# Where PE waits for VectorE's dots, and the order of the second stream in a two-layer transformer kernel

## The chip, the cores and the metric

One core of one Trainium2 chip runs the whole program in one launch. The metric is device time in microseconds (us), the median of several runs. The engines are named as the profile names them: PE is TensorE's matmul, PEld its weight load, DVE is VectorE, ACT is ScalarE, POOL is GpSimd, SP is SyncE, which here only issues DMAs. A "unit" is one 128 x 1024 block of weights in fp32, 512 KB.

## The reference, cut to what matters

The input is 256 tokens x and 256 context tokens ctx, of width 1024. Two layers of a first block are followed by two layers of a second one. The change lies between layer 0's MLP and layer 1's projection of the first block:

```python
mx = (silu(c) @ ada_w[i] + ada_b[i])[:, None, :]      # shift, scale, gate for x
mc = silu(c_ctx) @ ada_w[i] + ada_b[i]                # the same for ctx
hx = hx + gx2 * _mlp(_modulate(hx, norm2_g[i], sx2, cx2), mlp_w1[i], mlp_w2[i])
hc = hc + gc2 * _mlp(_modulate(hc, norm2_g[i], sc2, cc2), mlp_w1[i], mlp_w2[i])
# layer 1
ax = _modulate(hx, norm1_g[i], sx1, cx1)              # rms norm * (1 + scale) + shift
ac = _modulate(hc, norm1_g[i], sc1, cc1)
q, k, v = split(ax @ w_in)
cq, ck, cv = split(ac @ w_in)                         # layer 1 has no queries of ctx
q, k = rope(q), rope(k)
```

The queries of layer 1 are needed for x alone, its keys for x and ctx. Rope multiplies a tile by cosines and adds a copy with swapped rows times sines.

## The kernel before, in words

**Weights.** 284 units stream through four slots. SP loads a unit into `raw`; ACT rounds it to `whi` (L578); DVE subtracts to get the rest, `wlo` (L923); PE multiplies in three passes (L1663 to L1665: high x high, low x high, high x low), so that a tile of eight blocks is 24 matmuls. ACT and DVE each make unit u+3 in a step called `ahead(u)`, at a place in their own program that is written out by hand. Every engine works through its own list in order, and semaphores tie the lists together: `w_lo` counts finished units, `w_used` units that PE is through with.

**Two streams.** The activations `Hh`, `Hl` hold 512 columns, 256 of x ("first stream") and 256 of ctx ("second stream"). At the end of layer 0's MLP the last three tiles (`halves`, L1791 on) are done for x first, then for ctx, so that the norm of x can begin early. With halves (i, v), v = 0 for x and 1 for ctx, PE's order is (0,0), (1,0), (2,0), (0,1), then `sums_of(n, 0)` (L1769, the sums of squares of x, into PSUM bank 7), (1,1), `spread_of(n, 0)` (L1787), (2,1). The halves write to the banks 0, 1, 4 and 5, 2, 1.

**Dots.** Since layer 0's MLP leaves DVE time, DVE computes the modulation rows (`silu(c) @ ada_w`) there: `ada_dot` passes of 128 x 1024 (L997) whose elementwise product goes to PSUM banks 6 and 7. PE may not write to bank 7 before they are over. The last of them is followed by `ada_sums` (L1012), which raises `ada_ready`. PE waits for it before the first of the halves.

**Behind the dots.** DVE adds each finished half into X (L1319), ACT squares it (L628), POOL adds the squares (L1546, semaphore `sqx_used`); `sums_of(n, 0)` needs two of these adds and a last square. Then DVE scales (L1046, M tile), ACT adds the shift and rounds (`hi_x` L638 for x, `hi_c` L643 for ctx), DVE makes the low part (L1056), semaphores `low_x` and `nlo`, tile by tile, k = 0 to 7.

**Layer 1's projection.** It has 16 tiles in the order `L1_ORDER` (L103): 0 to 7 are queries of 256 columns, 8 to 15 keys of 512. `first_stream` (L1808) takes the first three tiles together as x's norm arrives; two more queries follow, then PE waits for all eight `nlo` (L2092) and does key 8. ACT evacuates tile i (`evac`, L672) from one of four PSUM banks into one of two buffers of `wk1` (`turned`), for which it waits until rope i-2 is over (`rope_out`); POOL multiplies by the cosines into the second half of the same buffer (L1619), DVE swaps, multiplies by the sines and adds (L1172, L1173, L1175). `L1_SECOND` says at which steps i of the 16 the second stream's tiles are made, on ACT and on DVE, and `L1_ROPES` at which steps DVE does which ropes. At step i ACT does `ahead`, the second stream's part, `evac(i)`; DVE does `ahead`, the second stream's part, the ropes.

The functions printed here are those that the change touches.

Of the kernel before, what the change touches and what calls it, by code (L numbers as in the profile page):

```python
# [28 lines left out]
ALU = mybir.AluOpType  # L29
# [5 lines left out]
KT = D // P  # L35
N = 256
# [5 lines left out]
QUARTERS = 4  # L42
# [23 lines left out]
U_L1 = U_L0_MLP + MLP_UNITS  # L66
L1_FM = 16
# [7 lines left out]
ADA_GROUPS = KT  # L75
# [24 lines left out]
OUT_BANKS = ((1, 2, 4), (5, 0, 3))  # L100
MLP_BANKS = ((0, 1, 4), (5, 2, 1))

L1_ORDER = (0, 1, 2, 3, 4, 8, 9, 10, 5, 11, 6, 12, 7, 13, 14, 15)  # L103


def program(nc, wall, aall, const, prm, xin, rpb, ali, out):
    with ExitStack() as top:
# [109 lines left out]
        class Norm:  # L217


            def __init__(self, src, n, T, width, streams, dst, eps=1e-6, keep=None, ready=None,  # L220
                         direct=False):
                self.src, self.n, self.T, self.width, self.eps = src, n, T, width, eps
                self.streams = streams
                self.dst = dst
                self.keep = keep
                self.ready = ready
                self.direct = direct

                self.pair = None
# [17 lines left out]
        norms = {}  # L247
# [41 lines left out]
        class Proj:  # L289
# [1 line left out]
            outs = 0  # L291
            ropes = 0

            def __init__(self, u0, tiles, high=False):
                self.u0, self.tiles = u0, tiles

                self.high = high
                self.o0, self.r0 = Proj.outs, Proj.ropes
                Proj.outs += len(tiles)
                Proj.ropes += sum(t.rope is not None for t in tiles)  # L300
# [2 lines left out]
                return (self.o0 + i) % 4 + (4 if self.high else 0)  # L303

            def turned(self, r):
                return wk2[:, 2 + r % 2, :] if self.high else wk1[:, r % 2, :]

            def swapped(self, r):
                return MO[:, r % 2, :] if self.high else wk1[:, 2 + r % 2, 0:N]
# [15 lines left out]

        L1_ROPES = ((), (), (0,), (1,), (2,), (3, 4)) + tuple((i - 1,) for i in range(6, L1_FM))
        L1_SECOND = (range(0, 4), range(4, 6), range(6, 8)) + (range(0),) * (L1_FM - 3)


        ROPE = {"q": (0, 128, C_COS, C_SIN), "m": (64, 128, C_COSM, C_SINM), "r": (0, 128, C_COSM, C_SINM),
# [6 lines left out]
        def v_place(o0, t):  # L339
# [4 lines left out]
            if o0 < V_L1 + 16:  # L344
# [1 line left out]
            return ps[:, (o0 + t) % 4, 0:N]  # L346

        p_l1 = Proj(U_L1, [Tile(256, "q", Q1[:, i, :], None, 0.125) if i < 8
                           else Tile(512, "q", K1[:, i - 8, 0:N], K1[:, i - 8, N:2 * N]) for i in L1_ORDER])

        def b2_tile(i):
            if i < 3 or 6 <= i < 8:
# [219 lines left out]
        def _(act):  # L572
# [73 lines left out]
            def last_halves(u, n):  # L646


                square(n, HALVED - 1)
                for k in range(HALVED, KT):  # L650
                    square_x(n, k)
                for k in range(HALVED, KT - 1):
                    ahead(u + k - HALVED + 1)
                    square_c(n, k)
                hi_x(n, 0)
                hi_x(n, 1)
                square_c(n, KT - 1)
                for k in range(2, KT):
                    hi_x(n, k)

            def evac(pr, i):
                t, o = pr.tiles[i], pr.o0 + i
                act.wait_ge(sem("w_used"), pr.u0 + i + 1)
                bank = ps[:, pr.bank(i), :]
                if t.rope is None:
                    act.activation(t.dst, bank[:, 0:t.T], ACT.Copy, scale=t.scale).then_inc(sem("proj_out"), 1)
                    return
                r = pr.rope_index(i)
                lo, hi, _, _ = ROPE[t.rope]
                if r >= 2:  # L670
                    act.wait_ge(sem("rope_out"), r - 1)
                ins = act.activation(pr.turned(r)[lo:hi, 0:N], bank[lo:hi, 0:N], ACT.Copy, scale=t.scale)  # L672
                if t.rest is not None:
                    rest = bank[0:64, 0:N] if t.rope == "m" else bank[:, N:2 * N]
                    ins = act.activation(t.rest, rest, ACT.Copy, scale=t.scale)
                ins.then_inc(sem("proj_out"), 1)
# [142 lines left out]


            for i in range(L1_FM):
                ahead(U_L1 + i)
                for k in L1_SECOND[i]:
                    hi_c(norms["l1a"], k)
                evac(p_l1, i)
# [86 lines left out]
        def _(dve):  # L912
# [251 lines left out]
            def rope(pr, i):  # L1164
                t = pr.tiles[i]
                r = pr.rope_index(i)
                lo, hi, _, sines = ROPE[t.rope]
                dve.wait_ge(sem("proj_out"), pr.o0 + i + 1)
                if r >= 2:
                    dve.wait_ge(sem("rope_out"), r - 1)  # L1170
                turned, swapped = pr.turned(r)[lo:hi, :], pr.swapped(r)[lo:hi, :]
                link(dve.stream_shuffle(swapped, turned[:, 0:N], SWAP))  # L1172
                link(dve.tensor_tensor(swapped, swapped, cst[lo:hi, sines:sines + N], ALU.mult))  # L1173
                dve.wait_ge(sem("rope_cos"), r + 1)
                dve.tensor_tensor(t.dst, turned[:, N:2 * N], swapped, ALU.add).then_inc(sem("rope_out"), 1)  # L1175

            def steps(pr, lo, hi):

# [344 lines left out]
        def _(pool):  # L1523
# [84 lines left out]
            def cosines(pr):  # L1608

                for i, t in enumerate(pr.tiles):  # L1610
                    if t.rope is None:
                        continue
                    r = pr.rope_index(i)
                    lo, hi, c, _ = ROPE[t.rope]
                    pool.wait_ge(sem("proj_out"), pr.o0 + i + 1)
                    if r >= 2:
                        pool.wait_ge(sem("rope_out"), r - 1)
                    turned = pr.turned(r)[lo:hi, :]
                    pool.tensor_tensor(turned[:, N:2 * N], turned[:, 0:N], cst[lo:hi, c:c + N], ALU.mult)\  # L1619
                        .then_inc(sem("rope_cos"), 1)  # L1620

            pool.wait_ge(sem("mhalf_set"), 1)
# [37 lines left out]
        def _(pe):  # L1660
# [129 lines left out]
            def halves(n, units, banks, x, free):  # L1790

                for v in range(2):
                    for i, u in enumerate(units):
                        if v == 0:
                            pe.wait_ge(sem("w_lo"), u + 1)
                        free(i, v)
                        for k in range(KT):
                            ins = mm3(ps[:, banks[v][i], 0:N], wtile(u % SLOTS, P * k, P),
                                      (x[0](k)[:, N * v:N * v + N], x[1](k)[:, N * v:N * v + N]), k == 0, k == KT - 1)
                        ins.then_inc(sem("w_used" if v else "half_used"), 1)  # L1800
                        if v == 1 and i == 0:
                            sums_of(n, 0)
                        if v == 1 and i == 1:
                            spread_of(n, 0)
# [23 lines left out]
                        if k == KT - 1:  # L1828
                            ins.then_inc(sem("w_used"), 1)

            def project(pr, lo, hi, x, kts=KT, ready=None):

                groups = [range(i, i + 1) for i in range(lo, hi)]
                if ready is not None:
                    groups = [range(0, TOGETHER)] + groups[TOGETHER:]
                for group in groups:
                    for i in group:
                        pe.wait_ge(sem("w_lo"), pr.u0 + i + 1)  # L1840
                        if pr.o0 + i >= 4:
                            pe.wait_ge(sem("proj_out"), pr.o0 + i - 3)
                    for k in range(kts):
                        if group[0] == 0 and ready is not None:
                            pe.wait_ge(sem("nlo"), ready + k + 1)
                        for i in group:
                            T = pr.tiles[i].T
                            ins = mm3(ps[:, pr.bank(i), 0:T], wtile((pr.u0 + i) % SLOTS, P * k, P),
                                      (x[0](k)[:, 0:T], x[1](k)[:, 0:T]), k == 0, k == kts - 1)
                            if k == kts - 1:  # L1850
                                ins.then_inc(sem("w_used"), 1)
# [128 lines left out]
            def mlp(u0, h0, T, ready, first=None, last=None):  # L1980
                def quarter(it, head=None, tail=None):
# [31 lines left out]

                    if tail is not None:
                        def free(i, v):
                            if v == 0 and i == 0:

                                pe.wait_ge(sem("ada_ready"), ADA_GROUPS + QUARTERS)
                            elif v == 1 and i == 1:
                                pe.wait_ge(sem("mlp_added"), 8 * it + (1 + h0 + HALVED))  # L2020
                            elif v == 1 and i == 2:
                                pe.wait_ge(sem("added_x"), 3 * tail.pair + 2)

                        halves(tail, range(u0 + 16 * it + 8 + HALVED, u0 + 16 * it + 16),
                               MLP_BANKS, (lambda k: HIDh[:, k, :], lambda k: HIDl[:, k, :]),
                               free)
# [62 lines left out]
            pe.wait_ge(sem("added_x"), 4)  # L2089
            first_stream(norms["l1a"], range(U_L1, U_L1 + TOGETHER), [(p_l1.o0 + i) % 4 for i in range(TOGETHER)], Hx)  # L2090
            project(p_l1, TOGETHER, L1_ORDER.index(8), Hx)
            pe.wait_ge(sem("nlo"), norms["l1a"].h0 + KT)  # L2092
            project(p_l1, L1_ORDER.index(8), L1_FM, Hx)
            for c in range(4):
                if c == 3:
                    pe.wait_ge(sem("rope_out"), p_l1.r0 + 16)
# [231 lines left out]
```

## Time and profile before

| | us |
|---|---|
| median of 3 runs | 1394.72 (1392.08 to 1395.4) |
| the profiled execution's own time | 1393.3 |
| its span in the trace | 1391.4 |
| PE busy in the span | 1322.6 (95%) |
| DVE, ACT, POOL busy | 993.6 (71%), 671.0 (48%), 193.1 (14%) |

The profile comes from one execution. Its span is 1.9 us shorter than that execution's own time, and that time is 1.4 us under the median of the runs. Times of single events are given in us from the span's start. PE is busy for 95% of the span; the page lists the rest as waits of single engines, and these are what a change to order can reach.

### The profile page before, as it was taken

The page shows a single profiled execution, that of the slowest core. Times are in us where ns is not written, and L with a number is a line of the kernel's source. Part 1 is how long each engine was busy: PE and PEld are TensorE (multiplying, and loading weights), DVE is VectorE, ACT ScalarE, POOL GpSimd, SP SyncE. Part 2 cuts the span into 40 slices and gives each one's busy share as a digit, 9 for nine tenths or more (in the row PEclk, how much of TensorE's full clock was granted, in tenths as well). Part 3 has the DMA queues.
Part 4 walks back from the last instruction along what each step waited for, and adds up shares of the span by engine and source line. Part 5 has one row for each costly group of instructions (what it writes and reads, how often), then busy time and mean ns, then how long its engine had stood idle before and what let it go on. Part 6 is the DMA issues. An engine that isn't in the chain of part 4 may idle for free. (4 is left out here: it accounts for less than half of the span.)

```text
span 1391.4 us, 24946 instructions
## 1 busy us (share of the span) xinstructions
PE 1322.6 (95%) x9374; PEld 1169.3 (84%) x9374; DVE 993.6 (71%) x1724; ACT 671.0 (48%) x1354; POOL 193.1 (14%) x280
## 2 busy tenths in 40 slices
PE   7999999999999999789999899999999989899987
PEld 6786679888888888688886899999899968899967
DVE  5698778898878878767439465565665976765974
ACT  4427743622414325144238464466455555465473
POOL 0101213000000000112006600000220016020034
PEclk8999999999999999899999999999999999899998
DMA  8782133567867868624320345655374533454511
GB/s 300 268 249 98 47 111 132 183 225 247 300 239 270 296 218 281 218 77 137 96 86 1 120 138 167 196 193 177 120 262 158 176 106 108 143 180 159 165 60 46
DMA packets 67666, 234.99 MB, mean 169 GB/s; under 512 B 7280, under 2 KB 12400, under 8 KB 67312
## 3 DMA queue, kind: packets, MB, share of 16 engines
q1 hardware_dynamic: 67568, 233.67, 49.8%
q8 instruction: 63, 1.03, 0.3%
q14 instruction: 35, 0.29, 0.1%
HBM read 232.59 MB, written 1.05 MB: 168 GB/s over the span
## 5 line engine op out<-in xcount | busy, mean ns | idle before, releaser
L923 DVE TENSOR_TENSOR wlo<-raw,whi 128x1024 fp32r<-128x1024 f32 x284 | 350.5, 1235 | 176.4 <-ACT whi L578 170.7
L578 ACT ACTIVATE whi<-raw 128x1024 fp32r<-128x1024 f32 x284 | 299.5, 1055 | 240.0 <-PE ps L1665 239.7
L1663 PE MATMUL ps<-Hh,whi 128*128 128x256 f32 (+1 forms) x896 | 304.7, 340 | 8.5 <-DVE Hl L1056 3.4
L1664 PE MATMUL ps<-Hl,whi 128*128 128x256 f32 (+1 forms) x896 | 301.0, 336 | 0.0
L1665 PE MATMUL ps<-Hh,wlo 128*128 128x256 f32 (+1 forms) x896 | 301.0, 336 | 0.0
L1663 PEld LDWEIGHTS ps<-Hh,whi 128*128 128x128 f32 x896 | 170.4, 190 | 31.2 <-issue 6.4
L1665 PEld LDWEIGHTS ps<-Hh,wlo 128*128 128x128 f32 x896 | 170.2, 190 | 19.2
L1663 PE MATMUL ps<-HIDh,whi 128*128 128x256 f32 (+1 forms) x536 | 177.8, 332 | 8.8 <-DVE ada L1012 8.8
L1664 PEld LDWEIGHTS ps<-Hl,whi 128*128 128x128 f32 x896 | 170.6, 190 | 18.3
L1663 PE MATMUL ps<-Gh,whi 128*128 128x256 f32 x624 | 178.1, 285 | 3.9 <-DVE Gl L1130 3.9
L1664 PE MATMUL ps<-HIDl,whi 128*128 128x256 f32 (+1 forms) x536 | 177.5, 331 | 0.0
L1665 PE MATMUL ps<-HIDh,wlo 128*128 128x256 f32 (+1 forms) x536 | 177.4, 331 | 0.0
L1664 PE MATMUL ps<-Gl,whi 128*128 128x256 f32 x624 | 176.9, 283 | 0.0
L1665 PE MATMUL ps<-Gh,wlo 128*128 128x256 f32 x624 | 176.8, 283 | 0.0
L997 DVE CUSTOM_DVE_ANT_0 ps<-aring,SB 128x1024 f32<-128x1024 f32 x112 | 141.3, 1261 | 2.6 <-DVE AC L997 0.3
L1663 PEld LDWEIGHTS ps<-Gh,whi 128*128 128x128 f32 x624 | 119.6, 192 | 5.0 <-issue 5.0
L1664 PEld LDWEIGHTS ps<-Gl,whi 128*128 128x128 f32 x624 | 119.6, 192 | 0.0
L1665 PEld LDWEIGHTS ps<-Gh,wlo 128*128 128x128 f32 x624 | 119.5, 192 | 0.0
L1663 PEld LDWEIGHTS ps<-HIDh,whi 128*128 128x128 f32 x536 | 102.9, 192 | 18.3 <-issue 9.2
L1664 PEld LDWEIGHTS ps<-HIDl,whi 128*128 128x128 f32 x536 | 102.9, 192 | 9.0
L1665 PEld LDWEIGHTS ps<-HIDh,wlo 128*128 128x128 f32 x536 | 102.9, 192 | 9.0
L696 ACT ACTIVATE wk<-ps,small 128x512 f32<-128x512 f32 (+2 forms) x160 | 84.2, 539 | 19.5 <-DVE small L1203 17.8
(251 smaller groups left out, 2041.5 us busy)
## 6 DMA issues: line engine op xcount, KB each, us to landing
raw<-wall SPq DMA_DIRECT2D x284, 512.0 KB, 4.2
aring<-aall SPq DMA_DIRECT2D x144, 512.0 KB, 4.6
AL<-ali SPq DMA_DIRECT2D x14, 192.0 KB, 5.2
X<-xin SPq DMA_DIRECT2D x2, 1024.0 KB, 7.4
BI<-rpb SPq DMA_DIRECT2D x4, 512.0 KB, 9.6
out<-X SPq DMA_DIRECT2D x4, 256.0 KB, 2.4
cst<-const SPq DMA_DIRECT2D x1, 960.0 KB, 8.3
par<-prm SPq DMA_DIRECT2D x1, 134.5 KB, 2.2
```

The costliest lines, as they stand in the source:

```text
L578: act.activation(whi[:, slot, :], raw[:, slot, :], ACT.Copy).then_inc(sem("w_hi"), 1)
L696: ins = act.activation(E[:, s % 2, r, c0:c0 + nk], ps[:, 2 * (s % 2) + r, c0:c0 + nk], ACT.Exp, bias=st[:, x:x + 1], accum_out=st[:, 4 + x ...
L923: dve.tensor_tensor(wlo[:, slot, :], raw[:, slot, :], whi[:, slot, :].bitcast(F32), ALU.subtract)\
L997: ins = dve.tensor_tensor_reduce(ps[:, 6:8, :].rearrange("p b n -> p (b n)"), w, SB[:, v, :], 1.0, start, ALU.mult, ALU.add, to)
L1663: pe.matmul(o, a[0], b[0], start=first, stop=False)
L1664: pe.matmul(o, a[0], b[1], start=False, stop=False)
L1665: return pe.matmul(o, a[1], b[0], start=False, stop=last)
```

## The change

It has two parts. First, PE's wait for `ada_ready` leaves the start of the halves and stands before `sums_of(n, 0)`. Second, layer 1's beginning is reordered: query 5 comes before key 8; ACT makes the high part of unit U_L1+3 behind x's `hi_x` tile k = 4, with the tiles 5 to 7 after it; the second stream's tiles are made at the steps 1 (two), 2 (two) and 3 (four) where they were made at 0 (four), 1 (two) and 2 (two); PE waits for them tile by tile within key 8; each tile is evacuated into its own place in Q1 or K1 and turned there, so that ACT's wait for rope i-2 goes, while the cosine product has still two buffers; and the ropes start at step 4 where they started at step 2.

```diff
-L1_ORDER = (0, 1, 2, 3, 4, 8, 9, 10, 5, 11, 6, 12, 7, 13, 14, 15)
+L1_ORDER = (0, 1, 2, 3, 4, 5, 8, 9, 10, 6, 11, 12, 7, 13, 14, 15)
...
             def turned(self, r):
+                if self.own:
+                    return self.tiles[r - self.r0].dst
                 return wk2[:, 2 + r % 2, :] if self.high else wk1[:, r % 2, :]
+
+            def cosined(self, r):
+                return wk1[:, r % 2, N:2 * N] if self.own else self.turned(r)[:, N:2 * N]
...
-        L1_ROPES = ((), (), (0,), (1,), (2,), (3, 4)) + tuple((i - 1,) for i in range(6, L1_FM))
-        L1_SECOND = (range(0, 4), range(4, 6), range(6, 8)) + (range(0),) * (L1_FM - 3)
+        L1_SECOND = (range(0), range(0, 2), range(2, 4), range(4, 8)) + (range(0),) * (L1_FM - 4)
+        L1_ROPES = ((), (), (), (), (0,), (1,), (2, 3), (4, 5), (6, 7)) + tuple((i - 1,) for i in range(9, L1_FM))
...
                 for k in range(2, KT):
                     hi_x(n, k)
+                    if n.pair == 1 and k == 4:
+                        ahead(u + 3)
...
-                if r >= 2:
+                if r >= 2 and not pr.own:
                     act.wait_ge(sem("rope_out"), r - 1)
...
             for i in range(L1_FM):
-                ahead(U_L1 + i)
+                if i:
+                    ahead(U_L1 + i)
...
-                dve.tensor_tensor(t.dst, turned[:, N:2 * N], swapped, ALU.add).then_inc(sem("rope_out"), 1)
+                dve.tensor_tensor(t.dst, pr.cosined(r)[lo:hi, :], swapped, ALU.add).then_inc(sem("rope_out"), 1)
...
-                    pool.tensor_tensor(turned[:, N:2 * N], turned[:, 0:N], cst[lo:hi, c:c + N], ALU.mult)\
+                    pool.tensor_tensor(pr.cosined(r)[lo:hi, :], turned[:, 0:N], cst[lo:hi, c:c + N], ALU.mult)\
...
                         if v == 1 and i == 0:
+                            if n.pair == 1:
+                                pe.wait_ge(sem("ada_ready"), ADA_GROUPS + QUARTERS)
                             sums_of(n, 0)
...
                         if group[0] == 0 and ready is not None:
                             pe.wait_ge(sem("nlo"), ready + k + 1)
+                        if second is not None:
+                            pe.wait_ge(sem("nlo"), second + k + 1)
...
                         def free(i, v):
-                            if v == 0 and i == 0:
-                                pe.wait_ge(sem("ada_ready"), ADA_GROUPS + QUARTERS)
-                            elif v == 1 and i == 1:
+                            if v == 1 and i == 1:
...
             project(p_l1, TOGETHER, L1_ORDER.index(8), Hx)
-            pe.wait_ge(sem("nlo"), norms["l1a"].h0 + KT)
-            project(p_l1, L1_ORDER.index(8), L1_FM, Hx)
+            project(p_l1, L1_ORDER.index(8), L1_ORDER.index(8) + 1, Hx, second=norms["l1a"].h0)
+            project(p_l1, L1_ORDER.index(8) + 1, L1_FM, Hx)
```

PE at the two places of the first part, before: the last tile of 512 columns ends, the halves begin; further down the sums stand behind the half (0,1). `HIDh` and `HIDl` are the MLP's hidden activations.

```order
2040 L1665 MATMUL ps<-HIDh,wlo 128x512
2041 L1663 MATMUL ps<-HIDh,whi 128x256 [waits ada_ready,w_lo]
2042 L1664 MATMUL ps<-HIDl,whi 128x256
...
2136 L1665 MATMUL ps<-HIDh,wlo 128x256
2137 L1769 MATMUL ps<-cst,RS 128x2 [waits sqx_used,modded]
2138 L1769 MATMUL ps<-cst,RS 128x2
```

and with the change:

```order
2040 L1677 MATMUL ps<-HIDh,wlo 128x512
2041 L1675 MATMUL ps<-HIDh,whi 128x256 [waits w_lo]
2042 L1676 MATMUL ps<-HIDl,whi 128x256
...
2136 L1677 MATMUL ps<-HIDh,wlo 128x256
2137 L1781 MATMUL ps<-cst,RS 128x2 [waits sqx_used,modded,ada_ready]
2138 L1781 MATMUL ps<-cst,RS 128x2
```

The wait for `ada_ready` has moved down by 96 matmuls; nothing else in this stretch has moved.

ACT from x's last `hi_x` tiles into layer 1's steps, before. `whi<-raw` is `ahead`, `Hh<-wk2 ... modded` the second stream, `wk1<-ps` (with the change `Q1<-ps`) the evacuation.

```order
326 L638 ACTIVATE Hh<-wk2,ada 128x256 [waits scaled_x] x6
327 L578 ACTIVATE whi<-raw 128x1024 [waits w_used,w_landed3]
328 L643 ACTIVATE Hh<-wk2,ada 128x256 [waits modded] x4
329 L672 ACTIVATE wk1<-ps 128x256 [waits rope_out,w_used]
330 L578 ACTIVATE whi<-raw 128x1024 [waits w_used,w_landed0]
331 L643 ACTIVATE Hh<-wk2,ada 128x256 [waits modded] x2
332 L672 ACTIVATE wk1<-ps 128x256 [waits rope_out,w_used]
333 L578 ACTIVATE whi<-raw 128x1024 [waits w_used,w_landed1]
334 L643 ACTIVATE Hh<-wk2,ada 128x256 [waits modded] x2
335 L672 ACTIVATE wk1<-ps 128x256 [waits rope_out,w_used]
```

and with the change:

```order
326 L647 ACTIVATE Hh<-wk2,ada 128x256 [waits scaled_x] x3
327 L587 ACTIVATE whi<-raw 128x1024 [waits w_used,w_landed3]
328 L647 ACTIVATE Hh<-wk2,ada 128x256 [waits scaled_x] x3
329 L683 ACTIVATE Q1<-ps 128x256 [waits w_used]
330 L587 ACTIVATE whi<-raw 128x1024 [waits w_used,w_landed0]
331 L652 ACTIVATE Hh<-wk2,ada 128x256 [waits modded] x2
332 L683 ACTIVATE Q1<-ps 128x256 [waits w_used]
333 L587 ACTIVATE whi<-raw 128x1024 [waits w_used,w_landed1]
334 L652 ACTIVATE Hh<-wk2,ada 128x256 [waits modded] x2
335 L683 ACTIVATE Q1<-ps 128x256 [waits w_used]
336 L587 ACTIVATE whi<-raw 128x1024 [waits w_used,w_landed2]
337 L652 ACTIVATE Hh<-wk2,ada 128x256 [waits modded] x4
```

One `whi` has moved up between x's tiles, the second stream's first group down behind the first evacuation, and its group of four is now the last.

DVE at the same place, with the change (before, one `wlo` stood at 791, the second stream in groups of 4, 2 and 2 behind it, and the first rope at 807, behind the third group):

```order
791 L935 TENSOR_TENSOR wlo<-raw,whi 128x1024 [waits w_hi] x2
792 L1058 SCALAR_TENSOR_TENSOR wk2<-X,SC,ps 128x256 [waits nlo,spread]
793 L1058 SCALAR_TENSOR_TENSOR wk2<-X,SC,ps 128x256 [waits nlo]
794 L1068 SCALAR_TENSOR_TENSOR Hl<-wk2,ada,Hh 128x256 [waits nhi] x2
795 L935 TENSOR_TENSOR wlo<-raw,whi 128x1024 [waits w_hi]
...
801 L1058 SCALAR_TENSOR_TENSOR wk2<-X,SC,ps 128x256 [waits nlo]
...
807 L935 TENSOR_TENSOR wlo<-raw,whi 128x1024 [waits w_hi]
808 L1184 STREAM_SHUFFLE wk1<-Q1 128x256 [waits rope_out,proj_out]
```

Two splits of weights stand in a row ahead of the second stream, the second of them waiting for ACT, with the whole second stream queued behind it.

## Rows read from the trace of the kernel before

**Rows 1.** The page: part 1, busy us of each engine; part 5, the dots' group, mean ns.

```profile
PE 1322.6 (95%) x9374; PEld 1169.3 (84%) x9374; DVE 993.6 (71%) x1724; ACT 671.0 (48%) x1354; POOL 193.1 (14%) x280
...
L997 DVE CUSTOM_DVE_ANT_0 ps<-aring,SB 128x1024 f32<-128x1024 f32 x112 | 141.3, 1261 | 2.6 <-DVE AC L997 0.3
```

**Rows 2.** PE's waits, 570 to 690: us in total, times, longest.

```profile
PE ps L1663 <- DVE ada L1012: 8.8, 1, 8.8
PE ps L1663 <- DVE Hl L1056: 3.0, 2, 2.6
```

**Rows 3.** Timeline of PE, 560 to 598: start, us, what, [idle before <-releaser].

```profile
573.71 0.39 PE L1665 MATMUL ps<-HIDh,wlo 128*128 128x512 f32 x1
582.90 0.55 PE L1663 MATMUL ps<-HIDh,whi 128*128 128x256 f32 x1 [8.80 <-DVE ada L1012]
...
588.75 0.28 PE L1663 MATMUL ps<-HIDh,whi 128*128 128x256 f32 x1
...
597.01 0.51 PE L1769 MATMUL ps<-cst,RS 128*128 128x2 f32 x4
```

**Rows 4.** Busy us (x instructions) of PE, PEld, DVE, ACT, POOL; granted clock; DMA.

```profile
574.00:582.90 8.90, 0.10 (x1) 0.03 (x1) 8.62 (x16) 1.61 (x2) 1.44 (x1) 0.75 0.72 249
582.90:588.60 5.70, 5.70 (x27) 5.70 (x28) 0.14 (x1) 0.00 (x0) 0.00 (x0) 0.50 0.00 0
...
604.40:624.30 19.90, 15.79 (x130) 15.39 (x130) 16.49 (x36) 10.47 (x20) 2.25 (x3) 1.00 0.27 89
624.30:678.00 53.70, 53.65 (x264) 44.52 (x264) 35.27 (x72) 19.26 (x33) 10.98 (x13) 1.00 0.41 134
```

**Rows 5.** Timeline of DVE, 573 to 589: a split, a dot, the sums, the first half.

```profile
573.13 1.22 DVE L923 TENSOR_TENSOR wlo<-raw,whi 128x1024 fp32r<-128x1024 f32 x1
...
576.37 2.11 DVE L997 CUSTOM_DVE_ANT_0 ps<-aring,SB 128x1024 f32<-128x1024 f32 x1
...
582.36 0.40 DVE L1012 TENSOR_TENSOR ada<-AC,par 128x4 f32<-128x4 f32 x4
588.47 0.48 DVE L1319 SCALAR_TENSOR_TENSOR X<-ps,ada,X 128x256 f32<-128x256 f32 x1 [5.71 <-PE ps L1665]
588.87 0.56 DVE L1023 SCALAR_TENSOR_TENSOR SC<-ada,par 128x8 f32<-128x8 f32 x3
```

**Rows 6.** Timeline of POOL and ACT: the last full add, then what follows the first half.

```profile
575.94 1.44 POOL L1540 TENSOR_TENSOR RS<-RS,wk 128x512 f32<-128x512 f32 x1 [4.00 <-ACT wk L605]
589.55 0.74 POOL L1546 TENSOR_TENSOR RS<-RS,wk 128x256 f32<-128x256 f32 x1 [12.16 <-ACT wk L628]
...
588.98 0.42 ACT L628 ACTIVATE wk<-X 128x256 f32<-128x256 f32 x1 [13.18 <-DVE X L1319]
```

**Rows 7.** Timeline of PE in layer 1: tile 3's first matmul, tile 4's, key 8's.

```profile
614.10 0.28 PE L1663 MATMUL ps<-Hh,whi 128*128 128x256 f32 x1
...
618.69 0.38 PE L1663 MATMUL ps<-Hh,whi 128*128 128x256 f32 x1 [1.58 <-DVE wlo L923]
...
624.35 0.50 PE L1663 MATMUL ps<-Hh,whi 128*128 128x512 f32 x1 [2.58 <-DVE Hl L1056]
```

**Rows 8.** Timeline of DVE there: splits, and the last low part between the first two.

```profile
611.50 1.23 DVE L923 TENSOR_TENSOR wlo<-raw,whi 128x1024 fp32r<-128x1024 f32 x1 [0.47 <-ACT whi L578]
...
616.19 0.49 DVE L1056 SCALAR_TENSOR_TENSOR Hl<-wk,ada,Hh 128x256 fp32r<-128x256 f32 x1 [0.18 <-ACT Hh L643]
617.41 1.23 DVE L923 TENSOR_TENSOR wlo<-raw,whi 128x1024 fp32r<-128x1024 f32 x1 [0.73 <-ACT whi L578]
...
621.22 1.23 DVE L923 TENSOR_TENSOR wlo<-raw,whi 128x1024 fp32r<-128x1024 f32 x1 [0.73 <-ACT whi L578]
```

**Rows 9.** Timeline of ACT: a high part released by PE; evacuation and high part.

```profile
597.27 1.06 ACT L578 ACTIVATE whi<-raw 128x1024 fp32r<-128x1024 f32 x1 [2.00 <-PE ps L1665]
...
616.06 0.37 ACT L672 ACTIVATE wk<-ps 128x256 f32<-128x256 f32 x1
616.33 1.05 ACT L578 ACTIVATE whi<-raw 128x1024 fp32r<-128x1024 f32 x1
```

More of the change, by code:

```diff
@@ L292, in program, with __init__ @@
             ropes = 0
-            def __init__(self, u0, tiles, high=False):
+            def __init__(self, u0, tiles, high=False, own=False):
                 self.u0, self.tiles = u0, tiles
+                self.own = own
                 self.high = high
@@ L348, in program @@
         p_l1 = Proj(U_L1, [Tile(256, "q", Q1[:, i, :], None, 0.125) if i < 8
-                           else Tile(512, "q", K1[:, i - 8, 0:N], K1[:, i - 8, N:2 * N]) for i in L1_ORDER])
+                           else Tile(512, "q", K1[:, i - 8, 0:N], K1[:, i - 8, N:2 * N]) for i in L1_ORDER], own=True)
         def b2_tile(i):
@@ L1829, in second_stream, with project @@
                             ins.then_inc(sem("w_used"), 1)
-            def project(pr, lo, hi, x, kts=KT, ready=None):
+            def project(pr, lo, hi, x, kts=KT, ready=None, second=None):
                 groups = [range(i, i + 1) for i in range(lo, hi)]
```

## The prediction

> **What bounds the kernel.** The page's first part shows PE busy for 1322.6 of 1391.4 us [rows 1]: the time is PE's work, its clock, and the few waits between. So I read PE's waits next, in the stretch that the change touches: one of 8.8 us for DVE's sums behind the dots, and shorter ones for DVE's low parts and splits [rows 2]. The timeline places them. PE's last matmul of 512 columns starts at 573.71, the halves at 582.90 [rows 3], just after DVE's sums, which start at 582.36 [rows 5]. The stretches show what the wait leaves behind: the granted clock, 1.00 (2.4 GHz) elsewhere, has a mean of 0.75 in the wait and is 0.50 (1.2 GHz) for the 5.70 us after it, in which 27 matmuls run [rows 4]. Last come layer 1's first tiles: tile 4 waits 1.58 us for its split, key 8 waits 2.58 us for the second stream [rows 7]. From 624.3 to 678.0 PE is busy for 53.65 of 53.70 us [rows 4], so whatever is saved before is kept there.
>
> **Part one, the moved wait.** Nothing else holds the halves at 574: the split of their last unit starts at 573.13 and takes 1.22 us [rows 5], and they write to no bank that the dots use. PE goes on one matmul of 512 columns later, 573.71 + 0.23 = 573.94 (53.65/264 us is the mean of mixed tiles; eight keys of 24 matmuls and three queries of 24 fit it at 0.234 and 0.120 us). Before the sums stand 96 matmuls of 256 columns. At full clock 96 - 27 = 69 of them took 597.01 - 588.75 = 8.26 us [rows 3, 4], 0.120 each, so all take 11.5 us and PE stands before its sums at 585.4.
>
> What is late next is DVE's chain. The sums of the dots end at 582.36 + 0.40 = 582.76 [rows 5], so `ada_ready`, now ahead of PE's sums, is up 2.7 us before PE gets there. But only then can DVE add its halves, and PE's sums need two of them squared and added by POOL. From rows: a half to the row scales 0.40, these 0.56 [rows 5]; a half's start to ACT's square 0.51, to POOL's add 1.08, which takes 0.74 [rows 5, 6]. The second half starts at 582.8 + 0.40 + 0.56 = 583.76 and its add is over at 583.76 + 1.08 + 0.74 = 585.6; the third half's square starts at about 584.7 and is over by then. PE starts its sums at 585.65, after a new wait of 0.2 us. They started at 597.01: **11.36 us**, of which 8.96 are the wait, 14.1 - 11.5 = 2.6 the low clock, less 0.2. All behind the sums (the spread, x's scaled tiles, the first stream) hangs on PE by the same order, and moves with it. The DMAs are no bound: in 582.90 to 588.60 their share is 0.00 [rows 4], so layer 1's first units have landed.
>
> POOL's two adds now run beside DVE's halves, with no row of the like before. If a half were held back for a whole add, the sums would start 0.74 later; if nothing, as above. I take the value above, since POOL's add begins only after the second half's start, and keep 0.74 for the range. For this a rule is at hand: a dot took 2.11 us from 576.37, where the mean is 1.26, beside POOL's add of 1.44 from 575.94 [rows 1, 5, 6]. The Trainium skill (SBUF — State Buffer, "SBUF: two separate sides") says that the pair of ports which DVE and GpSimd share is locked for a whole instruction, against DVE instructions with two SBUF inputs. The dot has two and agrees; a half reads X and a PSUM bank, so by the rule 0.2 stays, without it up to 0.9.
>
> **Part two, layer 1's start.** I keep the old clock here (all of it 11.36 earlier). Tile 3 starts at 614.10 [rows 7]. ACT's moved `whi` lies between `hi_x` tiles: it takes about 1.0 [rows 9] and delays the later ones by under 0.5, while PE asks for the last low part at 613.0 and DVE had it before its split at 611.50 [rows 8]; nothing.
>
> The next split, unit +4, sets the pace. ACT now evacuates tile 0 when the first stream is over for it. The last matmul of tile 0 starts at 614.10 - 7 x 0.12 = 613.27, that of tile 1 at 613.63; ACT starts 0.38 behind such a matmul (596.89 to 597.27) [rows 3, 9]. Evacuation at 613.65, `whi` at 614.01, the split 1.08 after (616.33 to 617.41) [rows 8, 9]: 615.09. From a split to the matmul that needs it is 1.28 (617.41 to 618.69) [rows 7, 8]. From one split to the next, with two tiles of the second stream, an evacuation and `whi` between, is 3.81 (617.41 to 621.22); with four tiles 5.91 (611.50 to 617.41) [rows 8]. A query takes 2.86, a key 5.63.
> - Tile 4: split ready 616.37, PE free 616.96: no wait (was 1.73 between slots, 1.58 of it idle).
> - Tile 5, a query: 615.09 + 3.81 + 1.28 = 620.18 against 619.82: waits 0.36.
> - Key 8: 622.71 + 1.28 = 623.99 against 623.04: waits 0.95 (was 2.73, 2.58 of it idle). Its last block is due at 623.99 + 7 x 0.70 = 628.9, and the last low part ends 5.18 after the split's start (611.50 to 616.68) [rows 8], at 627.9; no wait inside.
> - Key 9: 622.71 + 5.91 + 1.28 = 629.90 against 629.62: waits 0.28.
>
> Behind it DVE owes a split and one or two ropes a tile. Over the eleven tiles from 624.3 it is busy for 35.27 us [rows 4], 3.2 a tile; so the split for key 10 is there near 628.6 + 3.2 + 1.28 = 633.1 and needed at 635.5, and a key gives it 5.63 each. ACT's `rope_out` wait is gone, but PE was full there anyway: nothing. POOL's cosine products keep their two buffers: nothing, since their cover, the 5.63 - 3.2 = 2.4 us that DVE has left at each key, holds; without it a split would come late by one product at most, 0.74. So waits of 1.73 + 2.73 = 4.46 become 1.59: **2.87 us**.
>
> **Sum.** 11.36 + 2.87 = 14.2 us, against the profiled execution's own 1393.3: 1379.1. That execution is 1.4 under the median; the median becomes 1394.7 - 14.2 = **1380.5 us**. The runs before span 3.3 us, and under 0.3% (4.2 us) I would call no change.
>
> **Rivals.**
> - *The second part gives nothing* (0.14). The second stream begins later than before, and PE may again lose 4.46 us to splits and low parts at key 8. For it: PE waited on just these two. Against: the intervals above are of the same instructions. Only 11.4 remain: 1383.3.
> - *The clock falls at a short wait* (0.06). There are now four waits of 0.2 to 0.95 us in 45 us. Against it: two waits of 1.58 and 2.58 us left the granted clock at 1.00 [rows 4, 7]. A low stretch as after the long wait costs 2.6, and one or two of them give 1383 to 1386. The Trainium skill (TensorE: Matmul & The Clock Gate, "A second HAM failure mode: psum-queue depth-cycling") describes a kernel whose frequent short idles made the clock swing; the trace does not agree so far.
> - *The gain is not there* (0.05). Another wait of the same instruction stands behind `ada_ready`, or a later stage takes the time back. Waits and rows show none; 1391 to 1395.
> - *Slower* (0.02). The clock falls at tile 5's wait and stays at 0.50 over the projection. A low stretch loses 5.70 - 27 x 0.12 = 2.5 of 5.7 us, 0.43 of its length [rows 3, 4]; from 33 us on it eats the 14.2, and over the 59 us from tile 3 to the last key done wholly at half rate it costs 59: 1394.7 - 14.2 + 59 = 1440. Only the drop after 8.8 us of idleness speaks for it.
>
> **Numbers.** My forecast has 0.73. Below it: all waits in both parts gone gives 11.6 + 4.5 = 16.1, and 1.7 for the median's own scatter, 1377.0. Above it: the first rival with the same scatter, 1385.0. The two bounds leave out most of the clock rival and the last two. Faster takes the forecast, the first two rivals and a rest of the third: 0.94; same 0.04; slower 0.02.
>
> **What would show it.** Right: PE's row for the dots' wait gone, the first halves at about 573.9, granted clock 1.00 through 600, PE's sums at 585.7 released by POOL's add; tile 3 at about 602.7, waits of 0.4, 1.0 and 0.3 us ahead of tile 5, key 8 and key 9, all for a split; the last key's end some 14 us earlier. Wrong: a wait over 1 us at the sums, a granted clock under 1.00 there, waits for `Hl` inside key 8, or a wait behind 690 that was not there.

## The result, and the profile after

| | median us | range, runs | ratio to the kernel before (95%) |
|---|---|---|---|
| before | 1393.40 | 1390.37 to 1395.4, 4 | |
| with the change | 1377.84 | 1377.38 to 1378.86, 4 | 0.9897 (0.9882 to 0.9913) |
| the same again, in a later comparison | 1380.29 | 1378.84 to 1380.79, 4 | 0.9906 (0.9890 to 0.9922) |

The change makes the kernel 1.0% faster, 15.6 us in the first comparison and 12.8 in the second (1393.12 before). The forecast was 1380.5 us, 14.2 less than the median shown then.

The profiled execution took 1377.84 us, its span is 1375.8. First the page's part 1 [rows 1 before].

```profile
PE 1318.9 (96%) x9374; PEld 1165.9 (85%) x9374; DVE 993.8 (72%) x1724; ACT 670.2 (49%) x1354; POOL 196.7 (14%) x280
```

PE has done the same 9374 matmuls in 3.7 us less busy time. Most of that is the low clock, at which some of them no longer ran: the 96 matmuls between the dots' wait and the sums took 14.1 us and now take 11.5. PE's waits from 560 to 680, as in [rows 2]:

```profile
PE ps L1675 <- ACT K L686: 0.8, 1, 0.8
PE ps L1675 <- DVE wlo L935: 0.7, 1, 0.7
PE ps L1675 <- DVE Hl L1068: 0.4, 1, 0.4
PE ps L1781 <- POOL RS L1558: 0.2, 1, 0.2
```

The 8.8 us for the dots are gone, and of the waits for low parts only 0.4 is left, the one of the first stream. A wait of 0.7 us for a split stands at key 8, where tile 4 had one of 1.58 before [rows 7]; 0.2 for POOL's add is new; the 0.8 behind the last key was there before. By stretch, with the columns of [rows 4]: the halves to PE's sums, the sums to tile 3, tile 3 to key 8 (three queries), key 8 to the last key.

```profile
572.90:584.96 12.06, 11.88 (x99) 11.67 (x97) 10.84 (x23) 2.93 (x6) 2.96 (x3) 1.00 0.52 178
584.96:602.06 17.10, 16.72 (x140) 16.54 (x141) 12.16 (x24) 8.07 (x16) 4.41 (x4) 1.00 0.22 75
602.06:611.89 9.83, 9.05 (x75) 8.63 (x74) 7.08 (x12) 5.14 (x9) 1.52 (x2) 1.00 0.38 141
611.89:663.10 51.21, 51.18 (x240) 41.69 (x240) 37.51 (x80) 19.39 (x35) 14.15 (x13) 1.00 0.39 134
```

The granted clock is 1.00 in all four, where it was 0.50 for 5.70 us before. PE's own rows at the places of [rows 3, 7]: the first of the halves, the sums, the matmuls on both sides of the waits at tile 5, key 8 and key 9, and the first value matmul behind the last key, which stood at 678.87 before.

```profile
573.11 0.28 PE L1675 MATMUL ps<-HIDh,whi 128*128 128x256 f32 x1
...
584.96 0.58 PE L1781 MATMUL ps<-cst,RS 128*128 128x2 f32 x4 [0.18 <-POOL RS L1558]
...
607.71 0.28 PE L1677 MATMUL ps<-Hh,wlo 128*128 128x256 f32 x1
608.07 0.39 PE L1675 MATMUL ps<-Hh,whi 128*128 128x256 f32 x1
...
610.91 0.28 PE L1677 MATMUL ps<-Hh,wlo 128*128 128x256 f32 x1
611.89 0.50 PE L1675 MATMUL ps<-Hh,whi 128*128 128x512 f32 x1 [0.69 <-DVE wlo L935]
...
617.38 0.39 PE L1677 MATMUL ps<-Hh,wlo 128*128 128x512 f32 x1
617.79 0.50 PE L1675 MATMUL ps<-Hh,whi 128*128 128x512 f32 x1
...
663.95 0.36 PE L1675 MATMUL ps<-whi,Hh 128*128 128x256 f32 x1 [0.84 <-ACT K L686]
```

DVE and POOL ahead of the sums, as in [rows 5, 6]: the dots' sums, the first half, the second and third half in one row, and POOL's two adds.

```profile
581.57 0.40 DVE L1024 TENSOR_TENSOR ada<-AC,par 128x4 f32<-128x4 f32 x4
582.00 0.48 DVE L1331 SCALAR_TENSOR_TENSOR X<-ps,ada,X 128x256 f32<-128x256 f32 x1
...
583.00 0.88 DVE L1331 SCALAR_TENSOR_TENSOR X<-ps,ada,X 128x256 f32<-128x256 f32 x2
...
583.08 0.75 POOL L1558 TENSOR_TENSOR RS<-RS,wk 128x256 f32<-128x256 f32 x1 [6.49 <-ACT wk L637]
584.08 0.74 POOL L1558 TENSOR_TENSOR RS<-RS,wk 128x256 f32<-128x256 f32 x1 [0.25 <-ACT wk L637]
```

POOL's second add ends at 584.82, PE's sums begin 0.14 later. DVE's three splits in layer 1, as in [rows 8]:

```profile
602.98 1.23 DVE L935 TENSOR_TENSOR wlo<-raw,whi 128x1024 fp32r<-128x1024 f32 x1 [2.78 <-ACT whi L587]
...
606.79 1.23 DVE L935 TENSOR_TENSOR wlo<-raw,whi 128x1024 fp32r<-128x1024 f32 x1 [0.73 <-ACT whi L587]
...
610.61 1.23 DVE L935 TENSOR_TENSOR wlo<-raw,whi 128x1024 fp32r<-128x1024 f32 x1 [0.73 <-ACT whi L587]
```

The two executions started differently: the sums of the dots, before which nothing is changed, are at 582.36 before and at 581.57 after. So I compare by two stretches. **A** runs from the start of the dots' sums on DVE to PE's sums, **B** from there to the first value matmul. Both are starts in the timelines.

| kernel | dots' sums | PE's sums | value matmul | A | B | A + B |
|---|---|---|---|---|---|---|
| before | 582.36 | 597.01 | 678.87 | 14.65 | 81.86 | 96.51 |
| with the change | 581.57 | 584.96 | 663.95 | 3.39 | 78.99 | 82.38 |
| the same again | 583.47 | 586.85 | 665.84 | 3.38 | 78.99 | 82.37 |

A is 11.26 us shorter, B 2.87, together 14.13. Of the 15.6 between the spans, 0.79 lie ahead of A and 0.7 behind B, where nothing is changed. A and B come from one traced execution of each kernel.

### The profile page after: what moved, and what is told of

It is laid out like the page before. It is cut to its first block and busy times, and to the rows that moved or that the text cites. A ratio compares the mean times of both kernels' runs of the same rounds, so it can differ in the third digit from the quotient of the medians.

```text
span 1375.8 us, 24929 instructions
## 1 busy us (share of the span) xinstructions
PE 1318.9 (96%) x9374; PEld 1165.9 (85%) x9374; DVE 993.8 (72%) x1724; ACT 670.2 (49%) x1354; POOL 196.7 (14%) x280
```

## The experiments

Three theories stood: the terms add up as forecast (mine); the moved wait alone carries everything; the clock falls at the short waits that remain. A stretch in which the granted clock is 0.50 behind a wait is called a low stretch below, and its cost is the time beyond what the same matmuls take at 1.00.

### Each part alone

The wait alone is the kernel before with

```diff
                         if v == 1 and i == 0:
+                            if n.pair == 1:
+                                pe.wait_ge(sem("ada_ready"), ADA_GROUPS + QUARTERS)
                             sums_of(n, 0)
...
-                            if v == 0 and i == 0:
-                                pe.wait_ge(sem("ada_ready"), ADA_GROUPS + QUARTERS)
-                            elif v == 1 and i == 1:
+                            if v == 1 and i == 1:
```

> The kernel before with PE's wait for ada_ready moved to the sums and nothing else. My theory (the waits add up): PE's sums begin 11.2 us earlier against the dots than before, the clock stays at 1.00, layer 1's start keeps its waits of 1.6 and 2.6 us; 11.3 us under the kernel before, 2.9 above the full change. Rival (the low clock has another cause, or a wait behind takes it back): 8.9 or less.

The start alone is the full change with these lines taken back.

> The full change with PE's wait put back ahead of the halves. My theory: the 8.8 us wait and the low clock are back, layer 1's three waits are 0.2, 0.9 and 0.2 us as in the full change; 2.9 us under the kernel before. Rival (the second part needs the first, or gives nothing): 0.

| kernel | median us | ratio (95%) | dots' sums | PE's sums | value matmul | A | B |
|---|---|---|---|---|---|---|---|
| wait alone | 1383.40 | 0.9941 (0.9927 to 0.9954) | 582.49 | 585.87 | 670.65 | 3.38 | 84.78 |
| start alone | 1388.54 | 0.9971 (0.9959 to 0.9983) | 581.21 | 595.30 | 674.21 | 14.09 | 78.91 |

Each does to its own stretch what it should: A falls by 11.27 with the wait, B by 2.95 with the start. But the wait alone is only 8.35 (A + B) to 9.2 us (medians) faster, where 11.3 was expected, because its B is 2.9 longer than before. The start alone is 3.5 (A + B) to 4.0 us (medians) faster, where 2.9 was expected: its A is 0.56 shorter as well, by a shorter low stretch behind the same wait of 8.8 us. The stretches of the wait alone show why its B is longer: tile 4 and the wait at key 8, key 8, the rest.

```profile
607.60:613.29 5.69, 3.11 (x24) 2.91 (x24) 4.59 (x11) 3.03 (x6) 0.77 (x1) 0.95 0.44 130
613.29:619.40 6.11, 6.11 (x14) 4.79 (x15) 3.60 (x8) 2.15 (x4) 1.10 (x2) 0.50 0.30 108
619.40:670.60 51.20, 50.41 (x251) 41.86 (x249) 32.07 (x66) 17.85 (x33) 9.53 (x13) 1.00 0.38 127
```

The granted clock begins to fall in the wait of 2.55 us and is 0.50 for key 8's first 14 matmuls. They take 6.11 us, 2.8 more than at 0.2345 each. The kernel before has the same wait, 2.58 us, and kept 1.00 [rows 4, 7].

### The tiles turned in place, alone

The kernel before with `turned`, `cosined` and ACT's dropped rope wait as in the diff of the change, all orders as before.

> The kernel before with each tile of layer 1 turned in its own place, all orders as before. My theory: ACT's waits for ropes go (some 15 us in the trace before), but PE was full in that stretch and waits for second-stream tiles ahead of it; 0, within 1 us of the kernel before. Rival (ACT's rope waits held the splits back): the two waits at tile 4 and key 8 shrink, up to 2.5 us faster.

1393.70 us, ratio 1.0009 (0.9997 to 1.0021): no difference. In the trace A is 14.47 (583.00 to 597.47) and B 81.92 (to 679.39); PE's waits are those of before. By itself this is worth nothing. What it is for can be read from the lists: in the new order ACT would wait for rope 0 at tile 2, DVE does that rope behind the split of unit +7, and ACT makes the high part for that split only behind tile 3. The new order with the old buffers would stand still; it wasn't tried.

### Matmuls in the wait

```diff
                             if v == 0 and i == 0:
+                                u = (u0 + 16 * it + 8 + HALVED) % SLOTS
+                                for f in range(72):
+                                    pe.matmul(ps[:, MLP_BANKS[0][0], 0:N], whi[:, u, P * (f % KT):P * (f % KT) + P],
+                                              HIDh[:, f % KT, 0:N], start=(f == 0), stop=(f == 71))
                                 pe.wait_ge(sem("ada_ready"), ADA_GROUPS + QUARTERS)
```

> The kernel before with 72 extra matmuls of 256 columns (8.6 us, into a bank that is then overwritten) in PE's wait for the dots. My theory (the low clock comes from the idle wait alone): the halves start at the same place, at granted clock 1.00, the 96 matmuls take 11.5 instead of 14.1 us; 2.6 us under the kernel before. Rival (the clock falls anyway, or the halves are slow for another reason): 0.

1390.96 us, ratio 0.9990 (0.9981 to 0.9999). The filled wait, the 96 matmuls, then key 8's start and what follows:

```profile
573.60:582.20 8.60, 8.60 (x73) 8.57 (x71) 8.46 (x14) 1.62 (x2) 1.48 (x1) 1.00 0.73 251
582.50:594.10 11.60, 11.54 (x96) 11.54 (x97) 1.86 (x7) 1.25 (x3) 1.47 (x2) 1.00 0.01 2
621.50:626.00 4.50, 4.50 (x13) 3.57 (x14) 2.94 (x7) 1.33 (x2) 0.75 (x1) 0.65 0.17 65
626.00:677.00 51.00, 50.72 (x252) 42.08 (x250) 33.31 (x66) 18.14 (x32) 9.65 (x12) 1.00 0.40 134
```

The 96 matmuls take 11.6 us at granted clock 1.00, and A is 12.06 (582.11 to 594.17), 2.59 under the kernel before. So the low clock of [rows 4] comes from PE's idleness, and its price in that execution is the 2.6 of the forecast. The price varies: with the same wait of 8.8 us A is also 14.47, 14.10 and 14.09 (tiles turned, the kernel before again, the start alone), which is 2.4, 2.0 and 2.0 above 12.06. At key 8 the clock falls here too: B is 83.39 (to 677.56), 1.53 more. The filling is not the reason, since the kernel before can do the same without it (83.44, below). By the medians the filling gives 1.6 us where 2.6 was expected.

### The clock at key 8

`wait_only` again, with matmuls in the wait at key 8:

```diff
+            pe.wait_ge(sem("w_hi"), U_L1 + 6)
+            for f in range(20):
+                pe.matmul(ps[:, 4, 0:N], whi[:, (U_L1 + 5) % SLOTS, P * (f % KT):P * (f % KT) + P],
+                          Hh[:, f % KT, 0:N], start=(f == 0), stop=(f == 19))
             pe.wait_ge(sem("nlo"), norms["l1a"].h0 + KT)
```

> wait_only, and 20 extra matmuls of 256 columns (2.4 us, into a free bank) in PE's wait ahead of key 8. In wait_only's trace the granted clock falls to 0.50 in that wait and stays there until 619.4, which costs about 2.9 us; in the kernel before the same wait left it at 1.00. My theory (PE's idleness there makes it fall): granted clock 1.00 over key 8, 2.5 to 2.9 us under wait_only's 1383.4, at 1380.7. Rival (key 8 is slow for another reason, such as what DVE, ACT or a transfer do beside it): as wait_only.

A is 3.39 (582.91 to 586.30), B 81.99 (to 668.29), 2.8 under the wait alone and 0.1 off the kernel before; the granted clock stays at 1.00. A + B is 85.38, 11.13 less than before, near the first part's forecast of 11.36. This fits the theory that PE's idleness makes the clock fall, but does not show it for this place: of the five executions here with the same wait unfilled, the next one among them, two kept 1.00 as well (the kernel before, tiles turned), so one filled execution at 1.00 may be chance. The median, 1382.36 (0.9921, 0.9906 to 0.9935), is 1.0 under the wait alone's, which ran on another chip, and 1.7 above the 1380.7 expected.

Does the kernel before keep its clock there because of what precedes, or by how the run lies? A second profile of it:

> The kernel before, unchanged, for a second profile. Its first one has the granted clock at 1.00 behind the 2.6 us wait at key 8; wait_only and wait_filled have it at 0.50 there for up to 6 us. Theory (the fall is a matter of how the run lies, and the kernel before has it in some executions): either is possible; if it falls, the stretch from the dots' sums to the first value matmul is 96.5 + 2.5 = 99. Rival (what stands ahead of the wait decides, so it never falls here): 96.5.

```profile
617.00:622.00 5.00, 2.47 (x22) 2.27 (x20) 3.90 (x10) 2.79 (x6) 0.78 (x1) 1.00 0.44 141
622.00:626.40 4.40, 4.35 (x13) 3.39 (x13) 2.84 (x7) 1.33 (x2) 0.74 (x1) 0.64 0.20 78
```

The same kernel, the same wait of 2.58 us, and this time the clock falls behind it: B is 83.44 (594.71 to 678.15) against 81.86. Its A is 14.10 (from 580.61), 0.55 less, since the low stretch behind the dots' wait was shorter. So A + B of the kernel before is itself 96.51 in one execution and 97.54 in another. My 99 for this case was too much; the low stretch at key 8 cost 1.58 where I had put 2.5.

### How long a wait

The full change with the wait for `ada_ready` ahead of the second or the third of the halves, in `free`:

```diff
-                            if v == 1 and i == 1:
+                            if v == 0 and i == 1:
+                                pe.wait_ge(sem("ada_ready"), ADA_GROUPS + QUARTERS)
+                            elif v == 1 and i == 1:
```

> The full change with PE's wait for ada_ready ahead of the second of the halves. PE then waits 8.8 - 2.9 = 5.9 us there. Theory (the clock falls in a wait of this length as after 8.8): 5.9 of waiting and about 2.5 of low clock, so 8.6 - 0.2 above the full change. Rival (it holds): 5.9 above.

> The full change with PE's wait for ada_ready ahead of the third of the halves: 3.1 us of waiting there. Theory (2.6 us was enough in wait_only, so it falls): 3.1 + 2.5 = 5.4 above the full change. Rival (whether a short wait makes it fall hangs on where it lies, as between the kernel before and wait_only): 2.9 above, with the granted clock at 1.00.

| wait ahead of | median us | ratio (95%) | PE's wait | dots' sums | PE's sums | A | A over the full change |
|---|---|---|---|---|---|---|---|
| second half | 1386.12 | 0.9952 (0.9935 to 0.9970) | 5.96 | 582.42 | 593.60 | 11.18 | 7.79 |
| third half | 1381.61 | 0.9917 (0.9901 to 0.9933) | 3.10 | 582.04 | 590.97 | 8.93 | 5.54 |

For the third half the trace shows the wait, the low stretch and its end:

```profile
579.50:582.60 3.10, 0.01 (x1) 0.04 (x1) 3.00 (x9) 0.00 (x0) 0.00 (x0) 0.83 0.49 170
582.60:588.40 5.80, 5.80 (x27) 5.80 (x28) 1.56 (x6) 0.83 (x2) 1.47 (x2) 0.50 0.01 5
588.40:591.00 2.60, 2.60 (x24) 2.60 (x23) 0.18 (x1) 0.42 (x1) 0.00 (x0) 1.00 0.03 6
```

The excess is the wait less the 0.2 that it replaces and a low stretch: 5.96 - 0.2 + 2.0 and 3.10 - 0.2 + 2.6. B is that of the full change in both (78.91 and 78.92). The medians do not bear the excess out. Beside the full change's 1380.29 of the same comparison they are 5.8 us up for the second half, where 8.4 was expected and 5.9 by the rival, and 1.3 up for the third, where 5.4 and 2.9 were. So the traces show that the clock can fall behind these waits, and not that it mostly does. The profiled execution for the third half took 1386.42 us at a mean granted clock of 0.978, the other three 1381.05 to 1381.95 at 0.981. These have no trace here; that the wait left their clock alone would fit, and is not shown. It would explain 2.6 of some 5 us; behind B the profiled execution is another 2.6 us longer than the full change's first (714.41 against 711.85), and there nothing differs. That the fall comes in one execution and not in the next is shown for key 8's wait.

### The sixth query

`L1_ORDER` with key 8 ahead of query 5, the rest as in the change.

> The full change with key 8 back ahead of query 5, so five queries first. By the intervals of splits and low parts that held in the full change, key 8 then starts about 0.3 us after PE is free, but its last four low parts come at 2.4, 3.3, 4.2 and 4.9 us into it, where PE wants them at 2.8, 3.5, 4.2 and 4.9 minus the 2.9 us that a query would have covered. My theory: PE waits 2.4 us inside key 8 and in all 3 us from tile 5 to key 9, against 1.3 in the full change; 1.6 above it. Rival (the second stream is made in time anyway, the sixth query buys nothing): 0, within 0.5.

1381.48 us, ratio 0.9921 (0.9895 to 0.9948). The stretches are the wait inside key 8, the 12 matmuls that follow, and the rest:

```profile
612.00:614.20 2.20, 0.10 (x1) 0.00 (x0) 2.00 (x4) 0.91 (x2) 0.00 (x0) 1.00 0.26 47
614.20:618.80 4.60, 4.56 (x12) 3.31 (x13) 3.63 (x8) 3.45 (x6) 0.00 (x0) 0.64 0.23 92
618.80:667.00 48.20, 48.14 (x241) 40.02 (x239) 33.30 (x70) 15.28 (x28) 13.60 (x13) 1.00 0.39 131
```

PE waits 2.14 us for a low part inside key 8, as forecast, and pays with the clock as well, which was not. B is 81.91 (585.86 to 667.77), 2.9 more than with the change where 1.6 were expected. Some 1.75 of it is the low stretch (12 matmuls in 4.56 us, at 0.2345 each 2.81), the other 1.2 is waiting. So the sixth query's own part is 1.2 us, and the rest hangs on whether the clock falls, which it need not do in every execution.

### A step further

ACT's high parts a step ahead of the second stream:

```diff
             for i in range(L1_FM):
-                if i:
+                if i > 4:
                     ahead(U_L1 + i)
                 for k in L1_SECOND[i]:
                     hi_c(norms["l1a"], k)
                 evac(p_l1, i)
+                for j in ((1, 2), (3,), (4,))[i] if i < 3 else ():
+                    ahead(U_L1 + j)
```

> The full change with ACT's high part of each unit made one step earlier at layer 1's start, ahead of the second stream's tiles, so that DVE finds it done behind its low parts. In the full change DVE idles 0.73 us ahead of each of the splits for tile 5, key 8 and key 9. My theory: these idle times go, PE's waits of 0.24, 0.86 and 0.18 us with them; key 8's row shows no wait, layer 1's stretch from the dots' sums to the first value matmul is 82.4 - 1.3 = 81.1 us. Rival (ACT's high parts delay its second-stream tiles by as much): 82.4.

All three waits are gone; PE's rows show none between the first stream and the last key. B is 77.57 (586.19 to 663.76), 1.42 under the change, and A + B 80.97 against a forecast of 81.1. The median is 1377.56, ratio 0.9890 (0.9871 to 0.9910), the best of all here, but its interval holds the full change's 0.9897 and 0.9906. That it is better is shown by the stretch, in one trace, and not by the medians. One of its splits costs 1.76 us in place of 1.22, and PE did not wait for it; POOL's cosine product had begun 0.09 us before it:

```profile
607.21 1.76 DVE L937 TENSOR_TENSOR wlo<-raw,whi 128x1024 fp32r<-128x1024 f32 x1
...
607.12 0.78 POOL L1633 TENSOR_TENSOR wk<-Q,cst 128x256 f32<-128x256 f32 x1 [3.06 <-ACT Q L683]
```

## Why the prediction was right

**The moved wait, 11.36 forecast, 11.26 measured.** PE idled 0.18 us before its sums until POOL's second add let it go, where 0.2 was forecast, and the clock stayed at 1.00. The two terms were measured apart: filling the wait gave 2.59 for the clock against 2.6, so the rest of the 11.26 is the wait. That the clock's term came out to the hundredth is partly luck of the execution: both the forecast and this comparison rest on the profile of before in which the low stretch was the longest, and in three others it cost 2.0 to 2.4. POOL's adds did not hold DVE's halves back: two halves in 0.88 us, their usual 0.40 apart, beside an add of 0.75. The rule of the Trainium skill (SBUF — State Buffer, "SBUF: two separate sides") locks the shared ports against DVE instructions with two SBUF inputs; a half has one SBUF input and one in PSUM, and the trace agrees.

**Layer 1's start, 2.87 forecast, 2.87 measured.** The splits came 3.81 and 3.82 apart (602.98, 606.79, 610.61), against 3.81. The three waits were a little shorter than forecast: from start to start of matmuls, less one matmul's pace, 0.24, 0.86 and 0.18 in place of 0.36, 0.95 and 0.28. So 4.46 became 1.28, which would be 3.18. Of the 0.31 that is missing, some 0.2 went back into one more slow second matmul after a wait (0.1) and a slower pair of sums (0.06); the rest I have not placed. That the two numbers agree to the hundredth is luck, the more so as both stand for an execution of the kernel before whose clock held at key 8. Against the second profile of it, B is 4.45 shorter, and A + B 15.2 in place of 14.1.

**The edits costed at nothing.** Turning in place cost nothing, by its own kernel. ACT's moved high part was not run alone; that A + B comes out as summed leaves no room for more than 0.3 us.

**What the forecast had wrong is one premise.** It held against the clock rival that "two waits of 1.58 and 2.58 us left the granted clock at 1.00". That was one execution. In a second one of the same kernel the wait of 2.58 us was followed by a low stretch. The rival's condition was thus real, and it got 0.06. It did not come true: the change shortens just the wait at which it happens to 0.7 us, and in the five traces with the new start B is 78.91 to 78.99. This also means that the two parts are not independent, as my sum had them. The first rival, "the second part gives nothing", would have cost more than its 2.9 us where the clock then falls, as in the wait alone: 1383.4 us, near the 1383.3 written for it, by a mechanism it did not name.

**From 14.1 in the stretch to 15.6 and 12.8 in the medians.** For the second comparison I had expected 14 to 15 us, with 12 as the rival, if what each part alone gains in its medians simply adds; 12.8 lies between and does not decide. The first 580 us differ by up to 2.9 us between executions (the dots' sums stand at 580.61 to 583.47), and so do kernels with identical code there. Behind B, where nothing differs either, the rest of the span takes 710.75 us in one trace (the wait alone) and 714.54 in another (a step further). In 15 more runs of the kernel before the median is 1392.54, in 27 others 1392.56, so the 1394.7 from which the forecast counted was some 2 us high. Both stretches outside A and B scatter by more than the 1.5 us that at most lie between 14.1 and either median, and I put that difference down to them; where in them it arises was not looked for.

## What to carry to other kernels

Put a wait in front of the instruction that needs it, and then cost what stands next in line: here a wait of 8.8 us became one of 0.2 because the chain behind the dots (add, square, add) ended just as PE was through with its fourth half. Judge a wait of PE with the clock that follows it: those of 2.1 us and more seen here cost up to 2.8 us on top in some executions, and one profile does not say how often. Take such a profile twice before a forecast counts from it. Where a change is small against the scatter of whole runs, measure it between two events of the trace that enclose it and nothing else.

## What the runs showed of the hardware

**The granted clock after short idleness of PE is a matter of the execution.** Behind key 8's wait (2.55 to 2.58 us; 2.14 in the sixth query's kernel) and the third half's (3.10) the profiled executions kept 1.00 in two cases (before, turned in place) and fell to 0.50 in five (before again, wait alone, wait filled, sixth query, third half). Behind the waits of 5.96 and 8.8 us it fell each time, five times in all; behind the one of 1.57 or 1.58 us at tile 4, in six traces, and behind those of under 0.9 us it never did. The low stretches cost 1.5 to 2.8 us. What decides between the two outcomes is not shown. The Trainium skill (TensorE: Matmul & The Clock Gate, "A second HAM failure mode: psum-queue depth-cycling") describes a kernel whose frequent short idles made the clock swing. The traces here do not show that: the three waits of 0.18 to 0.86 us in a row left it at 1.00 in five traces, while a single one of 2.14 us was followed by 0.50.

**POOL is held by DVE's splits, and at times the other way round.** A cosine product of 128 x 256 takes 0.74 us while DVE is idle, and 1.60 where it starts during a split:

```profile
602.08 0.74 POOL L1631 TENSOR_TENSOR wk<-Q,cst 128x256 f32<-128x256 f32 x1 [5.44 <-ACT Q L683]
...
618.93 1.22 DVE L935 TENSOR_TENSOR wlo<-raw,whi 128x1024 fp32r<-128x1024 f32 x1
...
619.16 1.60 POOL L1631 TENSOR_TENSOR wk<-Q,cst 128x256 f32<-128x256 f32 x1 [12.50 <-DVE Q L1187]
...
623.04 0.48 DVE L1185 TENSOR_TENSOR wk<-wk,cst 128x256 f32<-128x256 f32 x1
624.12 0.74 POOL L1631 TENSOR_TENSOR wk<-Q,cst 128x256 f32<-128x256 f32 x1 [0.88 <-DVE Q L1187]
624.38 0.76 DVE L1185 TENSOR_TENSOR wk<-wk,cst 128x256 f32<-128x256 f32 x1
```

The split ends at 620.15, and the product 0.61 later, nearly its own length. The reverse stands at 624.38, where DVE's product with the sines starts during POOL's and takes 0.76 in place of 0.48, and in the split of 1.76 us above. Both agree with the exclusive lock on the shared ports that the Trainium skill describes (SBUF — State Buffer, "SBUF: two separate sides"). None of this delayed PE here: its rows show no wait behind these instructions.
